# Five modulation chunks by VectorE: multiply and add on VectorE during the first feed-forward, TensorE only sums over partitions

## The chip, the cores and the metric

The kernel runs on one core of a Trainium2 chip. The metric is the device time of one execution in microseconds (us); smaller is better. Engines are named as the profile names them: PE is TensorE, PEld its weight loads, DVE is VectorE, ACT is ScalarE, POOL is GpSimd, SP is SyncE, whose queue issues nearly all DMAs here.

## The reference

Two transformer blocks on 256 latent tokens (the first block also carries 256 context tokens), width 1024, all in float32. What matters here is the head of the first block: a modulation vector of nine chunks of 1024 is made from two conditioning vectors, and scales, shifts and gates the layers. Chunk 2 gates the first feed-forward, chunks 3 to 5 belong to the attention layer, chunks 6 to 8 to the second feed-forward.

```python
mod_lat = (jax.nn.silu(c) @ w_mod[layer] + b_mod[layer])[:, None, :]
mod_ctx = (jax.nn.silu(c_ctx) @ w_mod[layer] + b_mod[layer])[None, None, :]
ml = jnp.split(mod_lat, N_MOD, axis=-1)
mc = jnp.split(mod_ctx, N_MOD, axis=-1)
x = x + 0.5 * ml[2] * swiglu(modulate(rms_norm(x, norm1_g[layer]), ml[0], ml[1]),
                              ffn1_w_in[layer], ffn1_w_out[layer])
```

`w_mod` is 1024 x 9216, 37.7 MB, and it is used for two rows only. `swiglu` is 1024 to 2 x 2816 and back to 1024, on 512 tokens.

## The kernel before

Activations lie feature-major: 128 features of a chunk on the partitions, tokens in the free dimension. All large weights come as a stream of **units** of 1 MB (128 x 2048 floats) into the two buffers of `raw`. To keep float32 precision, each unit is split: ACT copies it to `w_hi` in a rounded format (L477), DVE subtracts to `w_lo` (L829), each in two halves of 1024 columns, and PE makes three matmuls for each product (L1455 hi by hi, L1456 hi by the activations' lo, L1457 lo by hi). In the first feed-forward (ffn1) a unit is 48 matmuls of 512 columns. It has 34 units in three slabs: 8 units of input weights and 4 of output weights, the same again, then 6 and 4. After an input unit k, ACT makes the silu (L563), DVE the product (L967), ACT its rounded part `h_hi` (L565), DVE `h_lo` (L970, which counts the unit as drained). After an output unit DVE adds to `x` (L929). DVE and ACT work on the halves of unit k + 2 around that: the first half before unit k's results, the second half behind them.

The modulation is computed in **mod units**: a quarter of a chunk, 256 rows of `w_mod`, 1 MB, laid out as 2 x 4 pieces of 256 columns. For each piece PE multiplies a 128 x 32 block of `sc_pad` (two columns are the silus of `c` and `c_ctx`, the others zero) with the piece, into 32 partitions of a bank of `ps_a`; four pieces fill four groups of 32 partitions (function `mod`, L1430). After the four quarters of a chunk DVE transposes the bank in 32 x 32 blocks and adds the bias (`modulation`, L850 and L853). There are 36 mod units. The first 8 (chunks 1 and 0) stand ahead of ffn1. Of the other 28, numbered n = 0 to 27, one each **rides** behind the units 0 to 20 of ffn1 on PE (`riding`), and the last 7 stand between ffn1 and the next projection. Mod units land in four slots (`wide_scr` and `scr`); SP issues the load of mod unit n right behind the load of stream unit n + 2 and waits there until PE has finished mod unit n - 4 (`mod_done`).

The order on each engine is the order of the code; nothing reorders it. DVE and SP run ffn1 in hardware loops over two units, PE has it written out. Semaphores that matter: `w_lo_ready` (a half of `w_lo` is there), `unit_drained`, `halves_done` (PE has finished a half), `mod_unit_done`, `mod_turned` (the bank is transposed and free).

## Time and profile before

| | |
|---|---|
| time, median of 3 runs | 1341.02 us (1337.63 to 1341.87) |
| profiled execution: span from first to last instruction | 1338.6 us |
| profiled execution: own time beside its span | not listed apart; the span is 2.4 us under the median and inside the range of the runs |
| PE busy | 1290.6 us, 96% of the span |
| DVE busy | 724.0 us, 54% |
| ACT busy | 588.0 us, 44% |
| mean granted PE clock | 0.977 of full speed |
| DMA | 214.17 MB, 160 GB/s in the mean |

Busy times are of one execution. A busy engine matters only where others wait for it, so the chain of waits and the time line of the stretch in question say more than these shares. ffn1 lies between about 40 and 428 us of the span.

### The profile page before, as it was taken

The numbers are of one execution on the slowest core, as the hardware profiler recorded it, in microseconds if no ns is written. First come the engines' busy times: TensorE is split into PE (matmuls) and PEld (weight loads), VectorE is DVE, ScalarE is ACT, GpSimd is POOL, SyncE is SP. The second block draws the span as 40 slices with busy tenths as digits, with TensorE's granted clock in tenths as the row PEclk, the third lists the DMA queues.
The fourth block names the chain that finished last, engine by engine and source line by source line (L and its number), as shares of the span: only waits on it lengthen the run. The fifth ranks groups of instructions, "written<-read, shape, count | busy, mean of one in ns | idle before, by whom it ended". The sixth has DMA issues, their size and how long they took to land.

```text
span 1338.6 us, 23359 instructions
## 1 busy us (share of the span) xinstructions
PE 1290.6 (96%) x8912; PEld 1147.0 (86%) x8912; DVE 724.0 (54%) x1210; ACT 588.0 (44%) x884; POOL 62.4 (5%) x72
## 2 busy tenths in 40 slices
PE   5899999999999999999998999998999999999997
PEld 3677777778887699888998999997888889999997
DVE  2533333333334765776665555655657767666664
ACT  2443223421233436554434656545434565544542
POOL 1000000000001000000001000002011201000001
PEclk7899999999999999999998999998999999999998
DMA  9544444344223344432453555544432325455542
GB/s 388 222 182 151 175 185 185 150 173 186 92 75 136 137 158 141 143 122 99 157 180 134 219 189 188 188 170 144 158 127 95 98 92 185 162 189 189 188 163 88
DMA packets 30958, 214.17 MB, mean 160 GB/s; under 512 B 3376, under 2 KB 4656, under 8 KB 5936
## 3 DMA queue, kind: packets, MB, share of 16 engines
q1 hardware_dynamic: 30032, 209.73, 43.3%
q10 hardware_dynamic: 864, 3.56, 0.7%
q8 instruction: 45, 0.74, 0.2%
q14 instruction: 17, 0.14, 0.0%
HBM read 212.23 MB, written 1.05 MB: 159 GB/s over the span
## 4 chain that ended last, share of the span: by engine, by line
PE 87%; DVE 5%; ACT 4%; DMA 2%; issue 2%; DVEq 0%; ACTq 0%; SPq 0%
PE ps_u L1455 26%; PE ps_u L1456 25%; PE ps_u L1457 25%; PE ps_a L1430 2%; PE ps_a L1413 1%; PE ps_a L1402 1%; DMA scr<-in_mods 1%; ACT w_hi L477 1%; DMA raw<-in_stream 1%; DVE w_lo L829 1%; PE ps_a L1668 1%; DVE sq L885 1%; PE ps_a L1605 1%; PE ps_a L1590 1%; PE ps_a L1764 1%
## 5 line engine op out<-in xcount | busy, mean ns | idle before, releaser
L1455 PE MATMUL ps_u<-x_hi,w_hi 128*128 128x256 f32 (+1 forms) x1744 | 545.5, 313 | 14.4 <-DVE x_lo L896 10.7
L829 DVE TENSOR_TENSOR w_lo<-raw,w_hi 128x1024 fp32r<-128x1024 f32 x322 | 394.4, 1229 | 289.7 <-ACT w_hi L477 285.3
L1456 PE MATMUL ps_u<-x_lo,w_hi 128*128 128x256 f32 (+1 forms) x1744 | 537.5, 308 | 0.0
L1457 PE MATMUL ps_u<-x_hi,w_lo 128*128 128x256 f32 (+1 forms) x1744 | 536.9, 308 | 0.0
L477 ACT ACTIVATE w_hi<-raw 128x1024 fp32r<-128x1024 f32 x322 | 336.9, 1054 | 301.4 <-PE ps_u L1457 253.7
L1455 PEld LDWEIGHTS ps_u<-x_hi,w_hi 128*128 128x128 f32 x1744 | 335.6, 192 | 44.2 <-issue 24.6
L1457 PEld LDWEIGHTS ps_u<-x_hi,w_lo 128*128 128x128 f32 x1744 | 335.5, 192 | 15.6
L1456 PEld LDWEIGHTS ps_u<-x_lo,w_hi 128*128 128x128 f32 x1744 | 335.8, 193 | 15.1 <-issue 0.5
L1455 PE MATMUL ps_u<-h_hi,w_hi 128*128 128x256 f32 (+1 forms) x800 | 246.4, 308 | 0.9 <-DVE h_lo L970 0.5
L1456 PE MATMUL ps_u<-h_lo,w_hi 128*128 128x256 f32 (+1 forms) x800 | 245.2, 307 | 0.0
L1457 PE MATMUL ps_u<-h_hi,w_lo 128*128 128x256 f32 (+1 forms) x800 | 245.0, 306 | 0.0
L1455 PEld LDWEIGHTS ps_u<-h_hi,w_hi 128*128 128x128 f32 x800 | 152.8, 191 | 11.0 <-issue 2.9
L1457 PEld LDWEIGHTS ps_u<-h_hi,w_lo 128*128 128x128 f32 x800 | 152.8, 191 | 7.0
L1456 PEld LDWEIGHTS ps_u<-h_lo,w_hi 128*128 128x128 f32 x800 | 152.8, 191 | 6.7
L408 POOL TENSOR_TENSOR sq<-sq 128x512 f32<-128x512 f32 (+1 forms) x30 | 36.7, 1222 | 974.2 <-ACT sq L529 886.9
L967 DVE TENSOR_TENSOR t<-s,ps_u 128x512 f32<-128x512 f32 (+1 forms) x44 | 24.4, 554 | 92.7 <-ACT s L563 92.7
L563 ACT ACTIVATE s<-ps_u 128x512 f32<-128x512 f32 (+1 forms) x44 | 21.5, 488 | 99.6 <-PE ps_u L1457 99.4
L929 DVE SCALAR_TENSOR_TENSOR x<-ps_u,gate_half,x 128x256 f32<-128x256 f32 x72 | 30.4, 477 | 32.6 <-PE ps_u L1457 32.5
L970 DVE TENSOR_TENSOR h_lo<-t,h_hi 128x512 f32 (+1 forms) x44 | 24.6, 559 | 36.1 <-ACT h_hi L565 36.1
L565 ACT ACTIVATE h_hi<-t 128x512 f32 (+1 forms) x44 | 23.1, 525 | 37.7 <-DVE t L967 37.7
L477 ACT ACT_TABLE_LOAD x19 | 24.4, 1283 | 17.9 <-DMA raw<-in_stream 17.7
L1430 PE MATMUL ps_a<-wide_scr,sc_pad 128*32 128x256 f32 x288 | 23.7, 463 | 7.1 <-ACT sc_pad L493 6.9
(228 smaller groups left out, 803.0 us busy)
## 6 DMA issues: line engine op xcount, KB each, us to landing
raw<-in_stream SPq DMA_DIRECT2D x153, 1024.0 KB, 4.8
wide_scr<-in_mods SPq DMA_DIRECT2D x18, 1024.0 KB, 6.7
scr<-in_mods SPq DMA_DIRECT2D x18, 1024.0 KB, 6.8
raw<-in_stream SPq DMA_DIRECT2D x8, 768.0 KB, 4.1
x<-in_tokens ACTq DMA_DIRECT2D x2, 1024.0 KB, 14.8
wide_scr<-in_cmp_w SPq DMA_DIRECT2D x2, 1024.0 KB, 7.8
sq<-in_cmp_w SPq DMA_DIRECT2D x2, 1024.0 KB, 7.5
out<-x SPq DMA_DIRECT2D x4, 256.0 KB, 2.2
```

What stands on the lines that cost most here:

```text
L408: pool.tensor_tensor(sq[:, 0, 0:width], sq[:, 0, 0:width], sq[:, kc, 0:width], ALU.add).then_inc(sq_sums, 1)
L477: act.activation(w_hi[:, k % 2, cols], raw[:, k % 2, cols], ACT.Copy).then_inc(h_ready, 1)
L563: act.activation(s1[:, j, 0:n], bank(k + j, 0, n), ACT.Silu).then_inc(silu_done, 1)
L565: act.activation(h_hi[:, 2 * p + j, 0:n], t1[:, j, 0:n], ACT.Copy).then_inc(hh_done, 1)
L829: dve.tensor_tensor(w_lo[:, k % 2, cols], raw[:, k % 2, cols], w_hi[:, k % 2, cols].bitcast(F32), ALU.subtract).then_inc(l_ready, 1)
L929: ins = dve.scalar_tensor_tensor(x[:, m + t, cols], bank(b, t, n)[:, cols], gate(m + t, s), x[:, m + t, cols], ALU.mult, ALU.add)
L967: dve.tensor_tensor(t1[:, j, 0:n], s1[:, j, 0:n], bank(k + j, 1, n), ALU.mult)\
L970: dve.tensor_tensor(h_lo[:, 2 * p + (first + j), 0:n], t1[:, j, 0:n], h_hi[:, 2 * p + (first + j), 0:n].bitcast(F32), ALU.subtract).then_i ...
L1430: ins = pe.matmul(ps_a[rows, b, 0:MOD_COLS], sc_pad[:, 2 * quarter + kc, :], mod_slots[slot][:, lo:lo + MOD_COLS], start=(quarter == 0 and ...
L1455: pe.matmul(dst, wh, xh, start=(kc == 0), stop=False)
L1456: pe.matmul(dst, wh, xl, start=False, stop=False)
L1457: ins = pe.matmul(dst, wl, xh, start=False, stop=(kc == span - 1))
```

## The change

Of the 28 mod units after the front, the first 20 (chunks 2 to 6, n = 0 to 19) are no longer multiplied by PE. Behind its work on unit n of ffn1, DVE multiplies each of the mod unit's two tiles of 128 x 1024 by the silu value of its partition, once for each of the two conditioning vectors, and adds to a running sum in `sq`, which is idle then (`mod_products`, four instructions of 1024 columns for a mod unit, eight tiles for a chunk). When a chunk's four quarters are in, PE sums over the partitions with 8 matmuls whose weights are a column of ones (`mod_sum`, `one_col`), one unit later than the last products. DVE reads the bank another unit later. Mod unit 20 rides on PE behind unit 22, the last seven stand where they stood. DVE and SP have ffn1 written out now, and `modulation` of chunks 2 to 6 moves from behind the loops into the sequence, at units 5, 9, 13, 17 and 21.

```diff
@@ -37,8 +37,9 @@
 MOD_QUARTERS = 4
 MOD_FRONT = 2 * MOD_QUARTERS
 MOD_RIDE = N_MOD * MOD_QUARTERS - MOD_FRONT
-MOD_LATE = 7
+MOD_SUMMED = 5 * MOD_QUARTERS
 MOD_ROWS = 32
+MOD_BANKS = (0, 1, 2, 0, 1)
 MOD_COLS = KD * MOD_ROWS
...
@@ -125,6 +126,7 @@
+        one_col = sb("one_col", [P, 2, MOD_ROWS])
...
@@ -166,6 +168,7 @@
+        mod_sums = sq[:].rearrange("p (b v k) n -> p b v (k n)", b=2, v=2)
...
@@ -356,22 +361,23 @@
                 sp.wait_ge(mod_done, u - 3)
                 mod_load(u, u - 4)
             load(0, 1, KD)
-            def riding_load(p, n):
-                sp.wait_ge(mod_done, 4 * p + (MOD_FRONT + n - 3))
-                mod_load(4 * p + (MOD_FRONT + n), n % 4)
-
-            with sp.Fori(0, MOD_RIDE // 4 - 1) as p:
-                for j in range(4):
-                    load(2 * p, 2 + j, KD)
-                    riding_load(p, j)
-            for n in range(MOD_RIDE - 4, MOD_RIDE):
+            def riding_load(n):
+                if n < 4:
+                    sp.wait_ge(mod_done, MOD_FRONT + n - 3)
+                elif n < MOD_SUMMED + 4:
+                    sp.wait_ge(mod_added, 4 * (n - 3))
+                else:
+                    sp.wait_ge(mod_done, MOD_FRONT + n - MOD_SUMMED - 3)
+                mod_load(MOD_FRONT + n, n % 4)
+
+            for n in range(MOD_RIDE):
                 load(0, 2 + n, KD)
-                if n == MOD_RIDE - 4:
-                    riding_load(0, n)
+                if n <= MOD_RIDE - 4:
+                    riding_load(n)
             units(2 + MOD_RIDE, 4, SLABS[2])
             units(FIRST["k"], 2)
             for n in range(MOD_RIDE - 3, MOD_RIDE):
-                riding_load(0, n)
+                riding_load(n)
             run(FIRST["k"] + 2, FIRST["ffn2"])
             def cmp_weights(i):
...
@@ -815,10 +821,13 @@
+            dve.memset(one_col[:], 0.0).then_inc(ones_ready, 1)
-            dve.wait_ge(ones_ready, 3)
+            dve.wait_ge(ones_ready, 4)
+            for v in range(2):
+                dve.memset(one_col[:, v, v:v + 1], 1.0).then_inc(ones_ready, 1)
...
@@ -844,9 +853,30 @@
             dve.tensor_tensor(gg[:], vec[:, V_F1:V_F1 + KD], vec[:, V_MIX:V_MIX + KD], ALU.mult).then_inc(vec_ready, 1)
             turned_cols = turned[:].rearrange("p (t c) -> p t c", c=MOD_ROWS)[:, :, 0:2]
+            def mod_products(n):
+
+                chunk, quarter = divmod(n, MOD_QUARTERS)
+                dve.wait_ge(mod_landed[n % 4], LANDED * (n // 4 + 3))
+                if quarter == 0 and chunk >= 2:
+                    dve.wait_ge(mod_summed, chunk - 1)
+                w = mod_slots[n % 4].rearrange("p (k c) -> p k c", k=2)
+                for kc in range(2):
+                    for v in range(2):
+                        total_v = mod_sums[:, chunk % 2, v, :]
+                        by = sc_pad[:, 2 * quarter + kc, v:v + 1]
+                        if quarter == 0 and kc == 0:
+                            ins = dve.tensor_scalar(total_v, w[:, kc, :], by, None, ALU.mult)
+                        else:
+                            dve.wait_ge(mod_added, 4 * n + 2 * kc + v - 1)
+                            ins = dve.scalar_tensor_tensor(total_v, w[:, kc, :], by, total_v, ALU.mult, ALU.add)
+                        ins.then_inc(mod_added, 1)
+
             def modulation(c, chunk, b):
-                dve.wait_ge(mod_done, MOD_QUARTERS * (c + 1))
+                if 2 <= c < 2 + MOD_SUMMED // MOD_QUARTERS:
+                    dve.wait_ge(mod_summed, c - 1)
+                else:
+                    dve.wait_ge(mod_done, MOD_QUARTERS * (c + 1) - (0 if c < 2 else MOD_SUMMED))
                 dve.transpose(turned[:], ps_a[:, b, 0:MOD_COLS]).then_inc(mod_turned, 1)
                 dve.wait_ge(mod_turned, c + 1)
                 cols = slice(chunk * KD, (chunk + 1) * KD)
...
@@ -959,39 +989,44 @@
                 def gate(m, s):
                     return gate_half[:, i, m, s:s + 1]
-                def pairs(pr, k, c, count, first=0):
+                def pair(pr, k, c, m, j):
+                    split(pr, k + 2, 0)
+                    dve.wait_ge(silu_done, c + 1)
+                    dve.tensor_tensor(t1[:, j, 0:n], s1[:, j, 0:n], bank(k, 1, n), ALU.mult).then_inc(prod_done, 1)
+                    dve.wait_ge(hh_done, c + 1)
+                    dve.tensor_tensor(h_lo[:, m, 0:n], t1[:, j, 0:n], h_hi[:, m, 0:n].bitcast(F32), ALU.subtract).then_inc(drained, 1)
+                    split(pr, k + 2, 1)
+
+                def pairs(pr, k, c, count):
                     with dve.Fori(0, count // 2) as p:
                         for j in range(2):
-                            split(pr + p, k + j + 2, 0)
-                            dve.wait_ge(silu_done, c + 2 * p + (j + 1))
-                            dve.tensor_tensor(t1[:, j, 0:n], s1[:, j, 0:n], bank(k + j, 1, n), ALU.mult)\
-                               .then_inc(prod_done, 1)
-                            dve.wait_ge(hh_done, c + 2 * p + (j + 1))
-                            dve.tensor_tensor(h_lo[:, 2 * p + (first + j), 0:n], t1[:, j, 0:n],
-                                              h_hi[:, 2 * p + (first + j), 0:n].bitcast(F32), ALU.subtract).then_inc(drained, 1)
-                            split(pr + p, k + j + 2, 1)
+                            pair(pr + p, k + j, c + 2 * p + j, 2 * p + j, j)
                 def outs(pr, k, last):
                     for o in range(4):
                         out_step(pr, k, o, n, gate, last)
                 if n == NB:
-                    pairs(0, base, count, 4)
-                    modulation(2, 2, 0)
-                    gates_of(0, 2)
-                    pairs(0, base + 4, count + 4, 4, 4)
-                    modulation(3, 3, 1)
-                    dve.wait_ge(gate_ready, 1)
-                    outs(0, base + 8, False)
-                    modulation(4, 4, 2)
-                    scale_of(1, 4, V_N2)
-                    pairs(0, base + 12, count + 8, 4)
-                    modulation(5, 5, 0)
-                    pairs(0, base + 16, count + 12, 4, 4)
-                    modulation(6, 6, 1)
-                    outs(0, base + 20, False)
-                    pairs(0, base + 24, count + 16, SLABS[2])
-                    outs(0, base + 30, True)
+                    at = 0
+                    for chunks in SLABS:
+                        for u in range(chunks + 4):
+                            if u < chunks:
+                                pair(0, base + at + u, count + u, u, u % 2)
+                            else:
+                                if u == chunks and at == 0:
+                                    dve.wait_ge(gate_ready, 1)
+                                out_step(0, base + at + chunks, u - chunks, n, gate, chunks == SLABS[2])
+                            if at + u < MOD_SUMMED:
+                                mod_products(at + u)
+                            c, late = divmod(at + u - 2, MOD_QUARTERS)
+                            if late == MOD_QUARTERS - 1 and 0 <= c < MOD_SUMMED // MOD_QUARTERS:
+                                modulation(2 + c, 2 + c, MOD_BANKS[c])
+                                if c == 0:
+                                    gates_of(0, 2)
+                                if c == 2:
+                                    scale_of(1, 4, V_N2)
+                        at += chunks + 4
+                        count += chunks
                 else:
                     with dve.Fori(0, 2) as s:
                         pairs(s * 6, base, s * 8 + count, SLABS[0])
...
@@ -1431,10 +1466,21 @@
                                         start=(quarter == 0 and kc == 0), stop=(quarter == MOD_QUARTERS - 1 and kc == 1))
                 ins.then_inc(mod_done, 1)
-            def riding(n):
+            def late(n):
                 u = MOD_FRONT + n
                 c = u // MOD_QUARTERS
-                mod(u, 1 if c == N_MOD - 1 else (c - 2) % 3 if c < N_MOD - 2 else 0, u % MOD_QUARTERS, n % 4, LANDED * (n // 4 + 3), c - 1)
+                mod(u, 1 if c == N_MOD - 1 else 0, u % MOD_QUARTERS, n % 4, LANDED * (n // 4 + 3), c - 1)
+
+            def mod_sum(c):
+
+                pe.wait_ge(mod_added, 4 * MOD_QUARTERS * (c + 1))
+                pe.wait_ge(mod_turned, c if c >= 3 else 2)
+                for v in range(2):
+                    for g in range(P // MOD_ROWS):
+                        rows = slice(g * MOD_ROWS, (g + 1) * MOD_ROWS)
+                        ins = pe.matmul(ps_a[rows, MOD_BANKS[c], 0:MOD_COLS], one_col[:, v, :],
+                                        mod_sums[:, c % 2, v, g * MOD_COLS:(g + 1) * MOD_COLS], start=(v == 0), stop=(v == 1))
+                ins.then_inc(mod_summed, 1)
             def unit(pr, k, operand, n=S, kcs=KD, ready=None, b=None, lag=2, parts=1):
...
@@ -1490,8 +1536,11 @@
                                 unit(0, base + k + o, from_x(n), n, ready=normed(i))
                             else:
                                 unit(0, base + k + o, from_h(n), n, chunks, ready=drained_at(0, base + k) if o == chunks else None)
-                            if k + o < MOD_RIDE - MOD_LATE:
-                                riding(k + o)
+                            c, behind = divmod(k + o - 1, MOD_QUARTERS)
+                            if behind == MOD_QUARTERS - 1 and c < MOD_SUMMED // MOD_QUARTERS:
+                                mod_sum(c)
+                            if k + o == MOD_SUMMED + 2:
+                                late(MOD_SUMMED)
                 else:
                     with pe.Fori(0, 2) as s:
                         slab(s, s * 6, base, SLABS[0])
```

PE, between unit 3 and unit 4 of ffn1. Before, the eight matmuls of mod unit 3 stand there:

```order
L1455 MATMUL ps_u<-x_hi,w_hi 128x512
L1456 MATMUL ps_u<-x_lo,w_hi 128x512
L1457 MATMUL ps_u<-x_hi,w_lo 128x512
L1430 MATMUL ps_a<-scr,sc_pad 32x256 [waits mod_landed3]
L1430 MATMUL ps_a<-scr,sc_pad 32x256 x7
L1455 MATMUL ps_u<-x_hi,w_hi 128x512 [waits x_lo_ready,w_lo_ready,unit_drained]
```

The same place now (L1501 to L1503 are the three matmul lines):

```order
L1501 MATMUL ps_u<-x_hi,w_hi 128x512
L1502 MATMUL ps_u<-x_lo,w_hi 128x512
L1503 MATMUL ps_u<-x_hi,w_lo 128x512
L1501 MATMUL ps_u<-x_hi,w_hi 128x512 [waits x_lo_ready,w_lo_ready,unit_drained]
L1502 MATMUL ps_u<-x_lo,w_hi 128x512
```

PE now, between unit 4 and unit 5, the first of the five places with a `mod_sum`:

```order
L1502 MATMUL ps_u<-x_lo,w_hi 128x512
L1503 MATMUL ps_u<-x_hi,w_lo 128x512
L1481 MATMUL ps_a<-sq,one_col 32x256 [waits mod_turned,mod_products_added]
L1481 MATMUL ps_a<-sq,one_col 32x256 x7
L1501 MATMUL ps_u<-x_hi,w_hi 128x512 [waits x_lo_ready,w_lo_ready,unit_drained]
L1502 MATMUL ps_u<-x_lo,w_hi 128x512
```

So eight short matmuls stand behind every fourth unit instead of behind each, and they wait for DVE's products where the old ones waited for a DMA.

DVE, one unit of ffn1 before (the body of its loop; `t` and `s` are the product and the silu, REGISTER_ALU and ISA rows compute the loop's semaphore values):

```order
L829 TENSOR_TENSOR w_lo<-raw,w_hi 128x1024 [waits w_hi_ready]
L967 TENSOR_TENSOR t<-s,ps_u 128x512 [waits silu_done]
L970 ISA [waits h_hi_done]
L970 TENSOR_TENSOR h_lo<-t,h_hi 128x512
L828 REGISTER_ALU
L829 TENSOR_TENSOR w_lo<-raw,w_hi 128x1024 [waits w_hi_ready]
```

DVE now, unit 5, where a transposition follows too (L838 is `w_lo`, L995 and L997 are `t` and `h_lo`):

```order
L838 TENSOR_TENSOR w_lo<-raw,w_hi 128x1024 [waits w_hi_ready,unit_drained]
L995 TENSOR_TENSOR t<-s,ps_u 128x512 [waits silu_done]
L997 TENSOR_TENSOR h_lo<-t,h_hi 128x512 [waits h_hi_done]
L838 TENSOR_TENSOR w_lo<-raw,w_hi 128x1024 [waits w_hi_ready]
L871 SCALAR_TENSOR_TENSOR sq<-wide_scr,sc_pad,sq 128x1024 [waits mod_products_added,mod_landed1]
L871 SCALAR_TENSOR_TENSOR sq<-wide_scr,sc_pad,sq 128x1024 [waits mod_products_added] x3
L880 STREAM_TRANSPOSE turned<-ps_a 128x256 [waits mod_chunk_summed]
L883 TENSOR_TENSOR mods<-turned,vec 128x16 [waits mod_turned]
L895 TENSOR_SCALAR gate_half<-mods 128x16 [waits mods_ready]
```

The four new instructions stand behind the second half of `w_lo` and ahead of the first half for the next unit but one. In a chunk's first quarter two of the four are TENSOR_SCALAR, without a sum to add to.

## Rows read from the trace of the kernel before

**Rows 1.** The page: span, PE busy, and the chain of waits by engine

```profile
span 1338.6 us, 23359 instructions
PE 1290.6 (96%) x8912; PEld 1147.0 (86%) x8912; DVE 724.0 (54%) x1210; ACT 588.0 (44%) x884; POOL 62.4 (5%) x72
...
PE 87%; DVE 5%; ACT 4%; DMA 2%; issue 2%; DVEq 0%; ACTq 0%; SPq 0%
```

**Rows 2.** Busy by stretch: from:to, length, PE, PEld, DVE, ACT, POOL, clock, DMA share, GB/s

```profile
60.00:150.00 90.00, 90.00 (x471) 69.56 (x470) 29.30 (x34) 31.45 (x35) 0.00 (x0) 1.00 0.48 185
```

**Rows 3.** Time line of PE at mod unit 0: start, duration, instruction

```profile
53.42 1.07 PE L1430 MATMUL ps_a<-wide_scr,sc_pad 128*32 128x256 f32 x16
54.42 0.50 PE L1455 MATMUL ps_u<-x_hi,w_hi 128*128 128x512 f32 x1
```

**Rows 4.** Time line of ACT: the silus behind units 0, 7, 24 and 29

```profile
53.53 0.60 ACT L563 ACTIVATE s<-ps_u 128x512 f32<-128x512 f32 x1 [3.08 <-PE ps_u L1457]
...
138.55 0.60 ACT L563 ACTIVATE s<-ps_u 128x512 f32<-128x512 f32 x1 [4.38 <-PE ps_u L1457]
...
341.25 0.60 ACT L563 ACTIVATE s<-ps_u 128x512 f32<-128x512 f32 x1 [4.38 <-PE ps_u L1457]
...
395.65 0.60 ACT L563 ACTIVATE s<-ps_u 128x512 f32<-128x512 f32 x1 [4.38 <-PE ps_u L1457]
```

**Rows 5.** Time line of PE: mod unit 21 and, back to back, 22 and 23

```profile
428.18 1.07 PE L1430 MATMUL ps_a<-wide_scr,sc_pad 128*32 128x256 f32 x16
...
429.07 1.91 PE L1430 MATMUL ps_a<-scr,sc_pad 128*32 128x256 f32 x32
```

**Rows 6.** Time line of DVE: behind unit 0, and the end of chunk 2's transposition

```profile
54.16 0.69 DVE L967 TENSOR_TENSOR t<-s,ps_u 128x512 f32<-128x512 f32 x1 [3.75 <-ACT s L563]
55.78 0.69 DVE L970 TENSOR_TENSOR h_lo<-t,h_hi 128x512 f32 x1 [0.93 <-ACT h_hi L565]
56.59 1.23 DVE L829 TENSOR_TENSOR w_lo<-raw,w_hi 128x1024 fp32r<-128x1024 f32 x1
61.33 1.23 DVE L829 TENSOR_TENSOR w_lo<-raw,w_hi 128x1024 fp32r<-128x1024 f32 x1 [3.51 <-ACT w_hi L477]
...
94.18 0.44 DVE L850 STREAM_TRANSPOSE turned<-ps_a 128x256 f32<-128x256 f32 x1
...
94.86 0.17 DVE L865 TENSOR_SCALAR gate_half<-mods 128x16 f32<-128x16 f32 x1
```

**Rows 7.** Groups of DVE by form, whole span: busy, mean ns of one, idle before

```profile
L829 DVE TENSOR_TENSOR w_lo<-raw,w_hi 128x1024 fp32r<-128x1024 f32 x322 | 394.4, 1229 | 289.7 <-ACT w_hi L477 285.3 <-DVE q_cur L1369 0.6
...
L970 DVE TENSOR_TENSOR h_lo<-t,h_hi 128x256 f32 x22 | 9.4, 426 | 15.7 <-ACT h_hi L565 15.7
...
L1114 DVE TENSOR_SCALAR scr<-scr,inv 128x512 f32<-128x512 f32 x16 | 7.1, 484 | 0.3
...
L1121 DVE SCALAR_TENSOR_TENSOR t<-u_pad,vec,t 128x256 f32<-128x256 f32 x8 | 3.9, 484 | 0.7 <-DVE t L1119 0.5
```

**Rows 8.** Time line of DVE: two halves of `w_lo` with no wait between

```profile
28.49 2.36 DVE L829 TENSOR_TENSOR w_lo<-raw,w_hi 128x1024 fp32r<-128x1024 f32 x2
```

**Rows 9.** Time line of PE around the `w_lo` at 61.33

```profile
60.26 0.39 PE L1456 MATMUL ps_u<-x_lo,w_hi 128*128 128x512 f32 x1
...
61.40 0.39 PE L1455 MATMUL ps_u<-x_hi,w_hi 128*128 128x512 f32 x1
...
62.53 0.39 PE L1457 MATMUL ps_u<-x_hi,w_lo 128*128 128x512 f32 x1
```

**Rows 10.** SP's issues behind unit 0, and DMA issues by line with KB and us to landing

```profile
57.99 0.33 SPq L336 DMA_DIRECT2D raw<-in_stream  x1
58.58 0.33 SPq L350 DMA_DIRECT2D scr<-in_mods  x1
...
raw<-in_stream SPq DMA_DIRECT2D x153, 1024.0 KB, 4.8
```

**Rows 11.** Time line at the start: PE's first mod matmuls

```profile
6.95 1.93 PE L1430 MATMUL ps_a<-wide_scr,sc_pad 128*32 128x256 f32 x16 [6.95 <-ACT sc_pad L493]
```

12 lines of the change are left out of this document (7 added, 5 removed).

## The prediction

> **What bounds the kernel now.** I read the page first: PE is busy for 1290.6 of 1338.6 us, and the chain that ended last runs over PE for 87% of the span [rows 1]. A busy PE alone would prove little, so I read the stretch that the change touches. From 60 to 150 us PE is busy for 90.00 of 90.00 us at a granted clock of 1.00, which is the 2.4 GHz level, while DVE is busy for 29.30 and ACT for 31.45 [rows 2]. The reader is to see one engine without a gap and two others with two thirds of their time free. In this stretch a microsecond taken from PE is a microsecond of the kernel, as long as nobody else becomes late.
>
> How PE's time divides shows in the silus of ACT, which follow the end of each input unit at once. From unit 0 to unit 7, each with a mod unit riding, seven periods take 138.55 - 53.53 = 85.02 us, 12.146 each. From unit 24 to unit 29, with no mod unit, five periods take 395.65 - 341.25 = 54.40, 10.88 each [rows 4]. The units are the same 48 matmuls, so a riding mod unit costs PE 12.146 - 10.88 = **1.266 us**. That is more than the 1.00 us from its first matmul to the next unit's first [rows 3], since the stream of large matmuls also stops and restarts; the difference of periods holds all of it.
>
> **What is removed and added on PE.** Before, 21 mod units ride in the first feed-forward; 20 of them go (n = 0 to 19), and the 21st stays, behind unit 22 instead of unit 20: moved, at the same price. Removed: 20 x 1.266 = 25.3 us. Added: five sums. Each has 8 matmuls of the same form, 32 output rows by 256 columns in four groups of partitions, and stands alone between two units like a mod unit. I take the same 1.266 us: 6.3 us. From below the bound is the cost where such blocks follow each other: 429.07 - 428.18 = 0.89 us [rows 5], in all 4.5 us. From above I add 1 us of waiting for each, in all 11.3 us. I take the price of the ride, because a sum interrupts the stream in just the way a ride does. Net: 25.3 - 6.3 = **19.0 us**, between 14.0 and 20.9.
>
> **What is added on DVE, and what hides it.** Let T be the end of a unit on PE, 53.42 for unit 0 [rows 3]. DVE then makes the product at T + 0.74, `h_lo` until T + 3.05 and the second half of `w_lo` until T + 4.40; after that it is idle until ACT's next `w_hi`, which lets it go on at T + 7.91 [rows 6]. The four new instructions go into that hole. There is no such row of 1024 columns. The nearest is `w_lo`, two inputs and 1024 columns: 1229 ns. A SCALAR_TENSOR_TENSOR with the scalar read from SBUF takes 484 ns for 256 columns where a TENSOR_TENSOR takes 426, so 58 ns more [rows 7]: 1.29 us for one. Two `w_lo` with no wait between take 2.36 us, so the second adds 1.13, 0.1 less than its duration [rows 8]; the pitch of the new ones is then 1.19 and the block of four 3 x 1.19 + 1.29 = 4.86 us. The bound from above is that the whole price goes with the width, 4 x 484 = 1.94 us each; the bound from below is 484 ns for a TENSOR_SCALAR of 512 columns, 0.97 us for twice that [rows 7], which 10 of the 80 instructions may well come near. I take 1.19, by the row of the same width.
>
> The block ends at T + 4.3 + 4.86 = T + 9.2. The transposition that follows at five places takes 95.03 - 94.18 = 0.85 us with its two small companions [rows 6]: T + 10.0. Then comes the first half of the next `w_lo`, 1.13 us: T + 10.3, or T + 11.2 at the five places. DVE's next product is due at 10.88 + 0.74 = T + 11.62. So DVE is on time in each unit, by 1.3 us, at the worst by 0.4. Even late it would not stop PE at once. PE's unit k + 2 needs `h_lo` of unit k, which is done at T + 3.05 and due at T + 10.88, so PE forgives about 7.8 us of lag.
>
> Three queues are touched by moved waits. **PE:** the sum of a chunk waits for the products of the unit before the last. They end at T + 9.2, and PE arrives at T + 10.88, so the wait is met 1.7 us early; behind it on PE stands the whole next unit, and everybody waits for that. **SP:** the load of mod unit n waits for the products of n - 4 instead of PE's mod unit n - 4, and the next stream load is queued behind it. SP comes to it at 58.58, right after the stream load at 57.99 [rows 10], T + 5.2 of unit n - 2, and the products of n - 4 were done over 17 us before. No change, also for the DMAs' times. The stream load at T + 4.6 lands after 4.8 us [rows 10] and ACT needs it in the middle of the unit after next, about T + 17.7, so the shorter period leaves 8 us. **DVE:** the transposition waits for a sum that PE made at least the length of a unit earlier.
>
> At nothing I cost the three more small memsets at the start (PE's first mod matmul comes at 6.95 us and waited for ACT [rows 11], far behind DVE's memsets), and the code written out where there were loops on DVE and SP; both have idle time ahead of their next wait. If that cover were gone, a few tenths of a microsecond would be at stake.
>
> Will a busier DVE slow PE's reads? Five matmuls from 60.26 to 61.40 take 1.14 us before the `w_lo` at 61.33, five from 61.40 to 62.53 take 1.13 under it [rows 9]. No.
>
> **The sum.** The profiled execution has a span of 1338.6 us, 2.4 under the median of the runs shown. 1338.6 - 19.0 = 1319.6 us of span; with the same 2.4 around it **1322.0 us**, which is 1341.02 - 19.0, 1.4% faster.
>
> **Rivals.**
> *TensorE waits for VectorE at the sums.* The 1.7 us of reserve vanish if the pitch passes (10.88 - 4.3) / 4 = 1.65 us, or if a block begins 1.7 us late. Against it: the idle time of DVE in [rows 6]. For it: the price of the new instruction is inferred from other widths. With 1 us for each of the five places the gain is 14.0 us: 1327 us.
>
> *VectorE becomes the bound, and the kernel slower.* A unit with no idle time costs DVE 1.13 + (56.59 + 1.23 - 54.16) = 4.79 us [rows 6, 8] and four pitches p. Twenty units and five transpositions: 20 x 4.79 + 5 x 0.85 + 80 p = 100 + 80 p. Less the 7.8 us of lag it must stay under PE's 20 x 10.88 + 6.3 = 223.9 us, so PE loses from p = 1.65, and the gain is used up at p = 1.88, where it reaches the 242.9 us of before. At the upper bound of 1.94 it is 247.4: 4.5 us slower, 1345.5 us. Against it stands the 1229 ns row, for it only that no wide SCALAR_TENSOR_TENSOR is in the trace.
>
> *Each VectorE instruction holds the next one for its own length again.* Then p = 2 x 1.29 = 2.58, DVE needs 100 + 206 - 7.8 = 298.6 us, and the kernel takes 1341 + 56 = 1397 us. The pair of `w_lo` in 2.36 us [rows 8] speaks against it: held like that it would take 3.7 or more. The Trainium skill, VectorE: DVE Perf Modes, section The DRAIN you can't avoid, says that a flush of roughly the duration less 266 ns follows every op and that the next op starts only then. By that rule, an estimate: p = 1.29 + 1.02 = 2.31, and the kernel would come out near 1375 us. The trace disagrees for two `w_lo` in a row.
>
> *The matmuls go, the time does not.* If something else paced the units, the weights for example, PE would wait where it now multiplies, and the time would stay at 1341. Against it: units 24 to 29 already run at 10.88 us with the same stream loads [rows 4], though with less DMA beside them.
>
> **How the numbers follow.** The forecast has 85 in 100. PE waiting at the sums has 6, DVE as the bound at its upper price 4, the doubled hold 2, no effect 3. The likeliest case alone runs from 1320 (sums at 0.89 us) to 1323; the runs of before lie up to 3.4 us under their median, so its low end is 1318. To the first rival the range reaches 1327. That leaves out 9 in 100 and what I have not thought of. About 0.3%, 4 us, is what a measurement of this kernel can tell from no change. Faster: 85 + 6 = 91; same: 3; slower: 4 + 2 = 6.
>
> **What the profile after would show.** Periods of 10.88 us between silus, and 12.15 where a sum stands; L1465 in 16 mod units (8 in front, 8 late) and L1481 in five blocks; L871 at about 1.29 us; DVE about 80% busy in the stretch and still with a short idle time ahead of each product; no wait of PE for DVE at L1481; the rest of the span 19 us earlier and otherwise the same. The prediction fails if L871 takes over 1.65 us, if L1481 shows a wait, or if the large matmuls are further apart than 0.227 us while DVE multiplies.

## The result, and the profile after

The changed kernel takes **1323.94 us** (median of 4 runs, 1322.94 to 1324.6), the kernel before 1340.9 on the same chip: a ratio of 0.9876, 95% interval 0.9863 to 0.9889. The forecast was 1322.0 in a range of 1318 to 1327. The profiled execution took 1324.6 us; its span is 15.8 us shorter than the one before [rows 1].

The page of the changed kernel: span, busy times, the chain by engine.

```profile
span 1322.8 us, 22749 instructions
...
PE 1273.7 (96%) x8688; PEld 1143.5 (86%) x8688; DVE 813.5 (61%) x1293; ACT 588.4 (44%) x884; POOL 62.6 (5%) x72
...
PE 88%; DVE 5%; ACT 3%; DMA 2%; issue 1%; DVEq 0%; SPq 0%; ACTq 0%
```

PE is busy for 16.9 us less, DVE for 89.5 us more, and DVE's share of the chain is what it was: the new work is paid out of idle time. Busy times by stretch, in the columns of [rows 2]:

```profile
60.00:150.00 90.00, 90.00 (x419) 73.12 (x418) 67.77 (x70) 32.97 (x37) 0.00 (x0) 1.00 0.51 196
415.00:419.00 4.00, 4.00 (x36) 2.05 (x36) 1.05 (x5) 0.26 (x1) 0.00 (x0) 0.57 1.01 426
739.00:744.00 5.00, 4.74 (x27) 4.77 (x28) 3.49 (x6) 2.97 (x5) 0.00 (x0) 0.66 0.43 139
910.00:928.00 18.00, 12.99 (x54) 11.36 (x55) 8.60 (x23) 6.85 (x16) 3.38 (x2) 0.53 0.18 60
```

In the first of them PE still has no gap, with DVE at 75%. The other three come back below. The time line of DVE behind unit 1 shows the block of new instructions and what stands around it (line 838 was 829, 995 was 967, 997 was 970):

```profile
65.58 0.69 DVE L995 TENSOR_TENSOR t<-s,ps_u 128x512 f32<-128x512 f32 x1 [3.63 <-ACT s L569]
67.07 0.69 DVE L997 TENSOR_TENSOR h_lo<-t,h_hi 128x512 fp32r<-128x512 f32 x1 [0.81 <-ACT h_hi L571]
68.02 1.23 DVE L838 TENSOR_TENSOR w_lo<-raw,w_hi 128x1024 fp32r<-128x1024 f32 x1 [0.26 <-ACT w_hi L483]
69.17 4.86 DVE L871 SCALAR_TENSOR_TENSOR sq<-wide_scr,sc_pad,sq 128x1024 f32<-128x1024 f32 x4
73.95 1.22 DVE L838 TENSOR_TENSOR w_lo<-raw,w_hi 128x1024 fp32r<-128x1024 f32 x1
76.46 0.69 DVE L995 TENSOR_TENSOR t<-s,ps_u 128x512 f32<-128x512 f32 x1 [1.29 <-ACT s L569]
```

The four take 4.86 us and begin without a wait; DVE then waits 1.29 us for the next silu. The instructions of lines 868, 871 and 1481 (min/median/max ns, first and last start us), and what PE waited for at 1481 (us, times):

```profile
L868 DVE TENSOR_SCALAR sq<-wide_scr,sc_pad x10: 746/747/748, 57.0 to 236.8; 128x1024 f32<-128x1024 f32 x10
L871 DVE SCALAR_TENSOR_TENSOR sq<-scr,sc_pad,sq x40: 1274/1278/1282, 80.0 to 273.7; 128x1024 f32<-128x1024 f32 x40
L1481 PE MATMUL ps_a<-sq,one_col x96: 379/379/404, 52.7 to 277.3; 128*32 128x256 f32 x96
  issue: 2.1, 6
```

The sums are not five but **six**: 96 records in blocks of 16, and the first stands at 52.70, ahead of every product; the one between units 4 and 5 is the second. The time line of PE shows it behind unit 0, and that of ACT gives the periods:

```profile
52.70 1.07 PE L1481 MATMUL ps_a<-sq,one_col 128*32 128x256 f32 x16
...
52.80 0.60 ACT L569 ACTIVATE s<-ps_u 128x512 f32<-128x512 f32 x1 [2.89 <-PE ps_u L1503]
64.95 0.60 ACT L569 ACTIVATE s<-ps_u 128x512 f32<-128x512 f32 x1 [4.38 <-PE ps_u L1503]
75.83 0.60 ACT L569 ACTIVATE s<-ps_u 128x512 f32<-128x512 f32 x1 [3.08 <-PE ps_u L1503]
...
377.19 0.60 ACT L569 ACTIVATE s<-ps_u 128x512 f32<-128x512 f32 x1 [4.38 <-PE ps_u L1503]
```

The period behind unit 0 is 12.15 us, the next 10.88. From the first to the last silu the feed-forward took 342.12 us [rows 4] and takes 324.39: 17.73 less, which is 14 x 1.266, for 20 rides removed and six sums added. The code says why. In `mod_sum`'s place PE asks, with `MOD_QUARTERS` = 4:

```python
c, behind = divmod(k + o - 1, MOD_QUARTERS)
if behind == MOD_QUARTERS - 1 and c < MOD_SUMMED // MOD_QUARTERS:
    mod_sum(c)
```

At k + o = 0 that is divmod(-1, 4) = (-1, 3), and the condition holds with c = -1. Eight matmuls sum a chunk that does not exist. I had read "one unit later than the last products" and counted chunks, not the cases in which the condition holds. The stray sum also advances `mod_summed` by one, so each of DVE's waits for a sum is already met by the sum before it. The data stay in order only because DVE's work on unit 4c + 5 waits for PE's results of that unit, which stand behind the sum of chunk c.

That leaves a second question. The feed-forward gave 17.73 us and the start 0.73 (this part is chance: the first silu starts between 52.16 and 53.96 us in the traces of this case, 53.50 and 52.75 in two of one and the same kernel), but the span fell by only 15.8. ACT has the same number of instructions in both kernels, so the start of one instruction in both, late in the program, gives what has been gained up to there. Time lines of ACT in the changed kernel, where the kernel before has the first of them at 439.31, the second at 757.60 and the third at 946.01:

```profile
420.86 1.31 ACT L525 ACTIVATE x_hi<-sq,mods 128x256 fp32r<-128x256 f32 x3 [5.27 <-DVE sq L915]
...
740.24 0.36 ACT L569 ACTIVATE s<-ps_u 128x256 f32<-128x256 f32 x1
...
930.69 1.06 ACT L483 ACTIVATE w_hi<-raw 128x1024 fp32r<-128x1024 f32 x1 [0.76 <-PE ps_u L1503]
```

Gained: 18.45 us, then 17.36, then 15.32. The gain gets lost in code that was not changed, and at places where the granted clock stands at its lower level (0.5, 1.2 GHz): the window from 739 to 744 shows 0.66, while before the window from 750 to 760, which holds the second instruction, had 1.00; and the low stretch from 910 to 928 is longer than its counterpart before (0.68 in the mean from 905 to 932, against 0.75 from 918 to 945). The low stretch at 415 loses nothing against the kernel before, which has the same one behind its own feed-forward:

```profile
433.00:437.00 4.00, 4.00 (x39) 2.04 (x38) 1.05 (x5) 0.26 (x1) 0.00 (x0) 0.58 1.01 426
```

### The profile page after: what moved, and what is told of

Its sections match the earlier page's. It is cut to its first block, busy times and chain, and to the rows that moved or that the text cites. A ratio compares the mean times of both kernels' runs of the same rounds, so it can differ in the third digit from the quotient of the medians.

```text
span 1322.8 us, 22749 instructions
## 1 busy us (share of the span) xinstructions
PE 1273.7 (96%) x8688; PEld 1143.5 (86%) x8688; DVE 813.5 (61%) x1293; ACT 588.4 (44%) x884; POOL 62.6 (5%) x72
## 3 DMA queue, kind: packets, MB, share of 16 engines
q10 hardware_dynamic: 864, 3.56, 0.7%
## 4 chain that ended last, share of the span: by engine, by line
PE 88%; DVE 5%; ACT 3%; DMA 2%; issue 1%; DVEq 0%; SPq 0%; ACTq 0%
PE ps_u L1501 26%; PE ps_u L1502 26%; PE ps_u L1503 26%; PE ps_a L1448 1%; PE ps_a L1437 1%; DMA scr<-in_mods 1%; PE ps_a L1717 1%; DMA raw<-in_stream 1%; DVE w_lo L838 1%; PE ps_a L1465 1%; ACT w_hi L483 1%; DVE sq L915 1%; PE ps_a L1654 1%; PE ps_a L1639 1%; PE ps_a L1813 1%
## 5 line engine op out<-in xcount | busy, mean ns | idle before, releaser
L1501 PE MATMUL ps_u<-x_hi,w_hi 128*128 128x256 f32 (+1 forms) x1744 | 544.2, 312 | 15.0 <-DVE x_lo L926 10.4
L1503 PE MATMUL ps_u<-x_hi,w_lo 128*128 128x256 f32 (+1 forms) x1744 | 537.4, 308 | 0.0
L838 DVE TENSOR_TENSOR w_lo<-raw,w_hi 128x1024 fp32r<-128x1024 f32 x322 | 393.8, 1227 | 220.1 <-ACT w_hi L483 218.4
L1501 PEld LDWEIGHTS ps_u<-x_hi,w_hi 128*128 128x128 f32 x1744 | 336.2, 193 | 39.7 <-issue 20.8
L1503 PEld LDWEIGHTS ps_u<-x_hi,w_lo 128*128 128x128 f32 x1744 | 336.3, 193 | 15.4
L1501 PE MATMUL ps_u<-h_hi,w_hi 128*128 128x256 f32 (+1 forms) x800 | 246.0, 308 | 0.7 <-DVE h_lo L1417 0.7
L1503 PE MATMUL ps_u<-h_hi,w_lo 128*128 128x256 f32 (+1 forms) x800 | 245.1, 306 | 0.0
L1501 PEld LDWEIGHTS ps_u<-h_hi,w_hi 128*128 128x128 f32 x800 | 152.8, 191 | 9.7 <-issue 2.2
L1503 PEld LDWEIGHTS ps_u<-h_hi,w_lo 128*128 128x128 f32 x800 | 152.8, 191 | 6.9
L995 DVE TENSOR_TENSOR t<-s,ps_u 128x512 f32<-128x512 f32 (+1 forms) x44 | 24.4, 554 | 65.3 <-ACT s L569 65.3
L871 DVE SCALAR_TENSOR_TENSOR sq<-scr,sc_pad,sq 128x1024 f32<-128x1024 f32 x40 | 48.7, 1278 | 0.0
L997 DVE TENSOR_TENSOR h_lo<-t,h_hi 128x512 fp32r<-128x512 f32 (+1 forms) x44 | 24.6, 559 | 33.3 <-ACT h_hi L571 33.3
L871 DVE SCALAR_TENSOR_TENSOR sq<-wide_scr,sc_pad,sq 128x1024 f32<-128x1024 f32 x30 | 36.7, 1278 | 0.0
```

Source lines behind the costliest of these rows:

```text
L838: dve.tensor_tensor(w_lo[:, k % 2, cols], raw[:, k % 2, cols], w_hi[:, k % 2, cols].bitcast(F32), ALU.subtract).then_inc(l_ready, 1)
L871: ins = dve.scalar_tensor_tensor(total_v, w[:, kc, :], by, total_v, ALU.mult, ALU.add)
L995: dve.tensor_tensor(t1[:, j, 0:n], s1[:, j, 0:n], bank(k, 1, n), ALU.mult).then_inc(prod_done, 1)
L997: dve.tensor_tensor(h_lo[:, m, 0:n], t1[:, j, 0:n], h_hi[:, m, 0:n].bitcast(F32), ALU.subtract).then_inc(drained, 1)
L1501: pe.matmul(dst, wh, xh, start=(kc == 0), stop=False)
L1503: ins = pe.matmul(dst, wl, xh, start=False, stop=(kc == span - 1))
```

## The experiments

Each was timed beside the kernel before, whose median then lay between 1337.7 and 1340.1; ratios are to that. Line numbers of an edited kernel can differ by a few.

**Five sums.** The condition becomes what the text of the change says.

```diff
-                            if behind == MOD_QUARTERS - 1 and c < MOD_SUMMED // MOD_QUARTERS:
+                            if behind == MOD_QUARTERS - 1 and 0 <= c < MOD_SUMMED // MOD_QUARTERS:
```

> The changed kernel makes six sums, not five: the condition for a sum also holds behind unit 0, for a chunk number of -1. Here it asks for a chunk number of at least 0, nothing else differs. Theory (a sum costs a ride's 1.27 us wherever it stands, even when it sums nothing useful): the period between the silus behind units 0 and 1 falls from 12.15 to 10.88 us, all the others stay, and the time falls by 1.3 us, to about 1322.7. Rival (the long first period is the start of the first feed-forward, not the sum): the period stays at 12.15 and so does the time.

Measured: 1318.26 us (1317.96 to 1319.31), ratio 0.9844 (0.9831 to 0.9858), span 1317.5. Its windows at the places above, its ACT instructions (those of the three rows above), and its first periods:

```profile
415.00:419.00 4.00, 2.89 (x34) 0.97 (x26) 2.20 (x7) 1.10 (x3) 0.00 (x0) 1.00 1.00 422
739.00:744.00 5.00, 5.00 (x44) 5.00 (x43) 1.60 (x2) 2.91 (x3) 0.00 (x0) 1.00 0.69 259
907.00:921.00 14.00, 10.42 (x43) 8.79 (x43) 6.13 (x20) 4.48 (x10) 1.69 (x2) 0.51 0.22 75
992.00:996.00 4.00, 3.38 (x17) 3.29 (x17) 3.97 (x10) 1.01 (x2) 3.61 (x4) 0.57 0.01 4
```

```profile
52.75 0.60 ACT L569 ACTIVATE s<-ps_u 128x512 f32<-128x512 f32 x1 [2.95 <-PE ps_u L1503]
63.63 0.60 ACT L569 ACTIVATE s<-ps_u 128x512 f32<-128x512 f32 x1 [4.37 <-PE ps_u L1503]
...
417.90 1.31 ACT L525 ACTIVATE x_hi<-sq,mods 128x256 fp32r<-128x256 f32 x3 [3.63 <-DVE sq L915]
...
736.36 0.36 ACT L569 ACTIVATE s<-ps_u 128x256 f32<-128x256 f32 x1
...
925.07 1.06 ACT L483 ACTIVATE w_hi<-raw 128x1024 fp32r<-128x1024 f32 x1 [0.71 <-PE ps_u L1503]
```

Behind unit 0 the period is 10.88 now: the sixth sum cost 1.27 us there. The whole is 5.7 us faster by the medians (4.3 by the ratios, since the kernel before also came out 1 us lower beside it), not 1.3. The changed kernel is behind it by 2.96 us at the first instruction, 3.88 at the second, 5.62 at the third. Beyond the 1.27 us, each step lies at a stretch where the changed kernel's clock was at 1.2 GHz and this one's was not, or not as long: the mod units and the statistics at 415 (0.57 against 1.00; DVE's `sq` there comes 1.64 us sooner for ACT), 739 to 744 (0.66 against 1.00), 18 us against 14 at 910. It has a low stretch at 992 that the changed kernel has not, and the spans at the end differ by 5.3 us. So 1.3 us of the 5.7 are work, and most of the rest goes with the clock. What the clock costs can be read from the same two mod units on PE, first in the kernel before, then in five sums:

```profile
433.68 3.56 PE L1430 MATMUL ps_a<-wide_scr,sc_pad 128*32 128x256 f32 x32
...
413.89 1.93 PE L1465 MATMUL ps_a<-wide_scr,sc_pad 128*32 128x256 f32 x32
```

That is 1.63 us. Five sums save it against the kernel before too, which makes their gain larger than the work taken away.

**The changed kernel and five sums, again.** Both as they were, timed side by side.

> The changed kernel unchanged, beside the other kernels of this call on one chip, since e1 came out 5.7 us faster than it and not 1.3, on another day's rows. Theory (beyond the 1.27 us of the sixth sum, the difference is TensorE's granted clock, which in the profile of the changed kernel was at 1.2 GHz for 3.4 us around 416 us and not in e1's, and longer around 910): 1322 to 1325 again, 4 to 6 us over five sums. Rival (a difference of chips): it comes within 2 us of the repeated e1.

> Five sums once more, beside the changed kernel. Theory: 1317 to 1320. Rival (chance): over 1321.

Measured: 1324.94 us (1321.67 to 1325.32), 0.9887 (0.9872 to 0.9902), and 1318.48 us (1317.83 to 1321.61), 0.9844 (0.983 to 0.9859). At two places the clock repeats with the kernel: from 415 to 419 it is 0.57 and 1.00, from 735 to 745 it is 0.83 and 1.00, as in the first executions. There it belongs to the kernel, not to one execution. It is not so further on: from 905 to 932 the changed kernel shows 0.68 in its first trace and 0.81 in this one, and five sums have no low stretch at 992 this time. Of the third step, and of the order in which single spans come out, a part is therefore chance of the execution. The difference itself is not: 6.5 us by the medians, 5.8 by the ratios.

**The sixth block elsewhere.** Five sums, and eight matmuls of the same form behind unit 21, for which nobody waits; their result is used by nobody.

```diff
+                            if k + o == MOD_SUMMED + 1:
+                                pe.wait_ge(mod_turned, 5)
+                                for v in range(2):
+                                    for g in range(P // MOD_ROWS):
+                                        rows = slice(g * MOD_ROWS, (g + 1) * MOD_ROWS)
+                                        pe.matmul(ps_a[rows, 2, 0:MOD_COLS], one_col[:, v, :],
+                                                  mod_sums[:, 0, v, g * MOD_COLS:(g + 1) * MOD_COLS], start=(v == 0), stop=(v == 1))
```

> Five sums' kernel with one block of the same eight matmuls more, but behind unit 21 instead of behind unit 0; its result is used nowhere. All that follows the first feed-forward is then shifted by 1.27 us, as in the changed kernel. Theory (the 1.27 us shift decides where TensorE's clock falls later, so the sixth sum costs 1.27 us directly and some 4 more through the clock): about 1324, with the clock at 1.2 GHz around 416 us and between 735 and 745 us. Rival (what costs the rest is the block's place behind unit 0): about 1319.7, with the clock at 2.4 GHz in both stretches.

Measured: 1325.23 us (1322.72 to 1325.92), 0.9899 (0.9879 to 0.9919). The time does not hang on the block's place behind unit 0: one such block costs 6.8 us against five sums again by the medians, 7.4 by the ratios. My theory was half right about the clock: from 415 to 419 it is 1.00 and not low, from 735 to 745 it is 0.83. In its profile, which is of its fastest execution, ACT also waits 2.7 us for a stream load, until 1142.7 us. So "the clock falls at 415" is not the whole of it; that the time ends up where the changed kernel's is, is shown, and by which stretches, differs.

**Each sum made twice.** The same eight matmuls again, into the same bank: the second time starts the bank anew (`start` for v = 0) and replaces the first, so the result is the same.

```diff
-                for v in range(2):
+                for v in (0, 1, 0, 1):
```

> Five sums' kernel with the eight matmuls of each sum made twice, back to back, into the same bank; the second time replaces the first. Theory (1.27 us is mostly the price of eight matmuls at 0.89 us, the rest that of the interruption, which is paid once): the five long periods grow by 0.89 us, from 12.15 to 13.04, and the time by 4.5 us, more or less what the clock does. Rival (the interruption is the price and matmuls pile up for little): they grow by less than 0.5 us.

Measured: 1322.52 us (1321.77 to 1326.76), 0.989 (0.9868 to 0.9912). The period with a sum goes from 12.15 to 12.96 us (silus at 96.05 and 109.01): another block of eight, right behind the first, costs 0.81, in all 4.1 us. The time is 4.0 us above five sums again, which was timed apart from it; by the ratios to the kernel before (0.989 against 0.9844) it is 6.2. Both are inside the intervals, so this run doesn't tell whether a shift of 4.1 us costs only what it adds. In its trace the clock is low around 420 us (0.83 from 415 to 425) and 1.00 from 735 to 745. The sixth block elsewhere was timed beside it, and there the kernel with 2.8 us less work on PE came out 2.7 us slower by the medians: work on PE alone does not order these kernels.

**All seven chunks.** `MOD_SUMMED = 7 * MOD_QUARTERS`, two banks more in the list, no late mod unit on PE, the loads of the last three in the loop with the others.

```diff
-MOD_SUMMED = 5 * MOD_QUARTERS
+MOD_SUMMED = 7 * MOD_QUARTERS
...
-MOD_BANKS = (0, 1, 2, 0, 1)
+MOD_BANKS = (0, 1, 2, 0, 1, 2, 0)
...
-            for n in itertools.islice(late_units, 3):
-                late(n)
             stat(1, 4)
-            for n in itertools.islice(late_units, 2):
-                late(n)
             spread(1, 4)
-            for n in late_units:
-                late(n)
```

> On top of five sums: all seven chunks behind the front go over VectorE, products behind units 0 to 27, sums behind every fourth unit up to 28, so TensorE has no mod unit between the first feed-forward and the next projection. In the feed-forward there are 7 sums at 1.27 us, one interruption more than with five sums and a ride. Theory (the late mod units lie on the path where the spread of the norm's roots stands behind two of them in TensorE's queue): the stretch from the last output unit to the first matmul of the projection, 13.1 us before, gets about 2 us shorter, and the time falls by 2 less 1.3, plus nothing else, to about 1321 to 1322. First rival (the late mod units only fill waits): the time goes up by one interruption, about 1323. Second rival (without them TensorE idles long enough for its clock to fall to 1.2 GHz there): a stretch at the low clock of some us more, time 1324 or more.

Measured: 1323.99 us (1322.61 to 1325.97), 0.989 (0.9874 to 0.9906), 5.7 slower than five sums, beside which it was timed, with less work on PE. Windows behind the feed-forward, and PE's time line there:

```profile
410.00:413.00 3.00, 0.67 (x3) 0.21 (x2) 2.29 (x5) 0.59 (x2) 0.00 (x0) 1.00 0.00 0
413.00:430.00 17.00, 12.45 (x39) 9.67 (x40) 9.77 (x27) 7.18 (x16) 0.00 (x0) 0.51 0.17 62
```

```profile
413.09 4.96 PE L1445 MATMUL ps_a<-ones,sq 128*128 128x1 f32 x24 [2.41 <-ACT sq L532]
```

The late mod units had filled the time in which PE waits for the statistics of the next norm. Without them PE idles 2.41 us, and what it does next runs at 1.2 GHz for 17 us.

**Six chunks.** The same edit with 6; of the last four mod units, three stand ahead of the statistics and one between them and their spreading.

```diff
-MOD_SUMMED = 5 * MOD_QUARTERS
+MOD_SUMMED = 6 * MOD_QUARTERS
...
-            late_units = iter(range(MOD_SUMMED + 1, MOD_RIDE))
+            late_units = iter(range(MOD_SUMMED, MOD_RIDE))
```

> Five sums' kernel, with chunk 7 over VectorE too: six sums, no ride, and of the seven late mod units on TensorE the four of chunk 8 stay. Three of them stand ahead of the statistics, where TensorE waits for the squares, and one, instead of two, ahead of the spread. In the feed-forward TensorE does the same as with five sums and one ride. Theory (seven chunks were slow because TensorE had nothing to do while it waited for the squares and its clock fell for 17 us): with the three units back the clock stays at 2.4 GHz there, and the time is that of five sums or 0.4 us less, since the spread no longer stands behind two units. Rival (VectorE's work in the last slab is what made seven chunks slow): two thirds of the loss stay, about 1322.

Measured: 1318.4 us (1317.66 to 1320.05), 0.9839 (0.9825 to 0.9852): the same as five sums. The clock fell here too, against the hope that one chunk's mod units would be cover enough:

```profile
412.00:415.00 3.00, 3.00 (x35) 2.40 (x34) 0.66 (x4) 0.26 (x1) 0.00 (x0) 1.00 0.76 248
415.00:426.00 11.00, 7.54 (x19) 4.77 (x16) 8.42 (x23) 6.11 (x12) 0.00 (x0) 0.53 0.07 28
```

**Half as much again on VectorE.** With five sums, behind each of the 80 new instructions one more of 512 columns, into a buffer that nobody reads then.

```diff
                         ins.then_inc(mod_added, 1)
+                        for e in range(1):
+                            at = (4 * n + 2 * kc + v) * 1 + e
+                            if at:
+                                dve.wait_ge(more_done, at)
+                            dve.scalar_tensor_tensor(q_cur[:].rearrange('p a n -> p (a n)'), w[:, kc, 0:NB], by, w[:, kc, NB:2 * NB], ALU.mult, ALU.add).then_inc(more_done, 1)
```

> Five sums, and behind each of the 80 products one more VectorE instruction of 512 columns whose result nobody uses: about 0.65 us of pitch each, 2.6 us a unit. VectorE then needs 100 + 80 x 1.19 - 5 (the 10 products without a sum are cheaper) + 52 = 242 us for the 20 units, more than TensorE's 224. Theory A, the prediction's (TensorE forgives 7.8 us of lag): TensorE loses 242 - 8 - 224 = 10 us in the feed-forward. Theory B (the sum forgives only the 1.7 us between the end of the products and the end of the next unit, and gives the lag back to TensorE at each of its places): TensorE loses about 16 us, and it waits at the sums, not at the units.

Measured once: 1348.63 us. From the first to the last silu 348.08 us instead of 323.12: 24.96 more, while the expectations had 10 and 16. The waits from 50 to 400 us (us in total, times, longest), and DVE's products at units 2 to 5:

```profile
PEld ps_a L1487 <- DVE sq L872: 16.0, 5, 4.0
PE ps_a L1487 <- DVE sq L872: 13.9, 5, 3.6
```

```profile
77.66 0.68 DVE L1001 TENSOR_TENSOR t<-s,ps_u 128x512 f32<-128x512 f32 x1
89.80 0.68 DVE L1001 TENSOR_TENSOR t<-s,ps_u 128x512 f32<-128x512 f32 x1
101.94 0.68 DVE L1001 TENSOR_TENSOR t<-s,ps_u 128x512 f32<-128x512 f32 x1
115.98 0.69 DVE L1001 TENSOR_TENSOR t<-s,ps_u 128x512 f32<-128x512 f32 x1 [2.90 <-ACT s L570]
```

DVE's period is 12.14 us, 1.3 longer than PE's. PE never waits for `h_lo` in this stretch; it waits at all five sums. At the first of them DVE's product, at 101.94, is 4 us late (the silu starts at 97.32, and the product follows a silu by 0.63 us when DVE is free), well under 7.8. And the wait has a second price, in the windows around the first of them:

```profile
98.00:100.00 2.00, 0.00 (x0) 0.00 (x0) 2.00 (x3) 0.00 (x0) 0.00 (x0) 0.91 0.99 418
100.00:106.00 6.00, 5.73 (x25) 3.69 (x26) 4.95 (x7) 1.58 (x2) 0.00 (x0) 0.50 0.00 1
```

After a wait of 3 us PE multiplies for 6 us at 1.2 GHz. That DVE itself waits 2.90 us for a silu behind the sum shows that it is PE that is slow by then. Four of the five waits last 3.0 to 3.6 us, and each has such a stretch behind it; the one before the sum at 199.44 us lasts 0.3, and the clock stays at 1.00. 13.9 us are the waits; I put the remaining 11 down to the four stretches at half the clock, 6 us or so each, and to the restarts.

**Twice as much on VectorE.** The same with two such instructions.

> Two more instructions behind each product: 5.2 us a unit more than with five sums alone. VectorE needs 100 + 95 - 5 + 104 = 294 us for the 20 units. Theory A: TensorE loses 294 - 8 - 224 = 62 us. Theory B: 68 us, with waits at the sums. Rival (the period of a unit is not set by VectorE's sum of work but by a chain through ScalarE, which waits for VectorE too): clearly more than 70 us.

Measured once: 1398.6 us, 77.2 more between the first and the last silu; expected were 62, 68 and over 70. Waits from 50 to 460 us, and two instructions of DVE at the ends of a block:

```profile
PE ps_a L1487 <- DVE sq L872: 53.5, 5, 14.7
PE ps_u L1507 <- DVE h_lo L1003: 10.0, 2, 5.3
...
72.40 1.28 DVE L872 SCALAR_TENSOR_TENSOR sq<-wide_scr,sc_pad,sq 128x1024 f32<-128x1024 f32 x1
...
82.98 1.22 DVE L839 TENSOR_TENSOR w_lo<-raw,w_hi 128x1024 fp32r<-128x1024 f32 x1
```

DVE is the bound for most of the stretch (busy for 82.80 of the 90 us from 60 to 150, PE for 75.26). A block of four products and eight extra instructions takes 82.98 - 72.40 = 10.58 us, so p is 2.65, and my formula 100 + 80p gives 312 us, 306 with the ten cheaper products counted as such. Against PE's 223.9 that is 82 us more, or 75 with 7.8 us forgiven; 77.2 lies between, so the total doesn't tell the two theories apart. The waits do: 53.5 us of them stand at the five sums and 10.0 at `h_lo`.

**The code written out, alone.** The kernel before with DVE's loops over pairs of units, in both feed-forwards, as loops of the generating program.

```diff
-                    with dve.Fori(0, count // 2) as p:
+                    for p in range(count // 2):
```

> The kernel before, only with VectorE's loops over the units of both feed-forwards written out. Theory (VectorE has idle time ahead of each wait, so loop arithmetic costs nothing): 1338 to 1341, ratio 1.000 with an interval around it. Rival (part of the change's gain comes from the written-out code): faster by 1 us or more, and shorter periods between silus than 12.146 us.

Measured: 1339.81 us (1336.72 to 1341.05, 11 runs), ratio 1.0001 (0.9991 to 1.001). It neither costs nor gives anything that could be measured.

**Rides and products.** VectorE makes all 80 products, PE rides all 20 mod units as before, and there is no sum; the products are used by nobody. The waits of SP and DVE are adapted; of the edit only PE's part is shown.

```diff
-                            c, behind = divmod(k + o - 1, MOD_QUARTERS)
-                            if behind == MOD_QUARTERS - 1 and c < MOD_SUMMED // MOD_QUARTERS:
-                                mod_sum(c)
+                            n_ride = k + o
+                            if n_ride < MOD_SUMMED:
+                                c = (MOD_FRONT + n_ride) // MOD_QUARTERS
+                                mod(MOD_FRONT + n_ride, (c - 2) % 3, n_ride % MOD_QUARTERS, n_ride % 4, LANDED * (n_ride // 4 + 3), c - 1)
```

> VectorE makes all 80 products as in the changed kernel, but TensorE still rides all 20 mod units and no sum is made; the products are used by nobody. Theory A (VectorE's 80 instructions of 1.28 us cost TensorE nothing, neither by waits nor by slower matmuls or copies): periods between silus 12.15 us as in the kernel before, the kernel as before, 1338 to 1342 us. Rival B (they cost something that the removal of the rides has hidden, through SBUF or through VectorE's lag): periods over 12.25 us, the kernel 1344 us or more.

Measured: 1340.52 us (1337.63 to 1343.14, 10 runs), ratio 1.0002 (0.9991 to 1.0012). The window shows PE without a gap and DVE with twice its work of [rows 2]:

```profile
60.00:150.00 90.00, 90.00 (x483) 69.05 (x481) 61.31 (x63) 31.05 (x35) 0.00 (x0) 1.00 0.47 178
```

The first period is 12.15 us (silus at 52.16 and 64.31), as before. So the whole load on VectorE is free here, and the gain of the change is what leaves PE. That it is free at the shorter period too is shown by the changed kernel: its 10.88 us with products is that of the units without a mod unit before [rows 4].

## Why the prediction was right, and where it was not

**The mechanism was right, and so were the sizes.** PE had no gap in the stretch, work taken from it came back in full as shorter periods, and DVE's new work went into its idle time. A block on PE costs 1.27 us when it stands alone, a ride (the 17.73 us) as well as a sum (12.15 less 10.88). A wide product takes 1278 ns where I had 1290, four take 4.86 us as forecast, and the block ends at 69.17 + 4.86 = 74.03, 9.2 us after unit 1's end, which is 0.11 before the silu at 64.95, as in [rows 3, 4]. DVE's reserve of 1.3 us is there in the row at 76.46. The large matmuls stay 0.227 us apart while DVE multiplies (23 pitches from 68.83 to 74.04 us). DVE is busy for 75% of the stretch where I had about 80%: the two first products of each chunk, 747 ns, are cheaper.

**"Added: five sums" was mis-sized.** It was six: 7.6 us in place of 6.3, and 17.7 in place of 19.0. The row at 52.70 shows the sixth, and five sums show what it costs directly. The statement that there are five blocks at L1481 fell with it.

**"The rest of the span 19 us earlier and otherwise the same" failed.** Of 18.45 us gained, 3.1 were gone at 930 us. I had no term for the clock. The two spans differ by 15.8 us, the medians by 17.0; how much of the 3.1 us a typical execution loses, the single profiles don't tell. The loss at 740 is in both traces of the changed kernel, the longer stretch at 910 in one of them.

**That 1322.0 came within 2 us is partly luck.** The forecast was added up for five sums. The kernel with five sums takes 1318.3 us, at the very edge of the range; by the ratio (0.9844) it gains 20.9 us where I had 19.0, and 1.6 of that comes from the low stretch at 415, which the kernel before has and it has not. The sixth sum and the clock, neither of which I had thought of, brought the changed kernel back up to near the forecast, on its other side. The upper part of the range was meant for waits at the sums, and there were none.

**"PE forgives 7.8 us of lag" was wrong.** That holds for the wait on `h_lo` alone. The sum of a chunk needs the products of the unit before, and there the reserve is 1.7 us (T + 10.88 less T + 9.2), as the same paragraph had it for the wait. The two extra-work kernels show the lag paid mostly at the sums (13.9 us of waits there and none at `h_lo`, then 53.5 and 10.0). For this change it made no difference, since DVE was never late; but the turning point of the second rival was off: without the 7.8 us it lies at p = (223.9 - 100) / 80 = 1.55, not 1.65.

**The rivals.** No wait of PE for DVE stands at L1481 in the changed kernel, so the first did not happen, and with p = 1.19 nor did the second. The third, the doubled hold, is out: with it four products would take 3 x 2.56 + 1.28 = 8.96 us, and 4.86 are measured. The Trainium skill, VectorE: DVE Perf Modes, section The DRAIN you can't avoid, would put the starts of two such products 2.3 us apart (an estimate from its "duration less 266 ns") if each were held until the flush is over. The same section also says that a next op which is not held starts earlier, which the prediction left out; the trace shows such an earlier start, with (4.86 - 1.28) / 3 = 1.19 us from start to start. The fourth, no effect, is contradicted by the silus at 10.88.

**What was costed at nothing was nothing.** DVE's written-out code (ratio 1.0001) is shown alone. VectorE's load beside the matmuls is shown with everything else of the change but the sums and the missing rides, SP's written-out code, its waits and the memsets included (1.0002), so none of these costs anything that could be measured, unless two of them cancel.

**The better version.** Five sums, 1318.3 and 1318.5 us, beats the kernel before by 1.6% and the changed one by 0.4 to 0.5%. Six chunks are as fast and no faster.

**What stays open.** Why a shift of 1.3 us in the feed-forward brings the lower clock at 415 or 740 (both in the changed kernel, 740 alone with the block behind unit 21), while one of 4.1 us has it around 420 and not at 740, and costs 4.0 to 6.2 in all. That the clock differs there is shown; what tips it is not, and no run set the clock by itself. For the sixth block elsewhere the profile has a low stretch at 740 and one late stream load, and I can't divide the 7 us between them.

## What to carry to other kernels

Count instructions added by a condition by running through its first and last cases, or count them in the build, not by the sentence that describes them; `divmod` of a negative number is one such case. A reserve is that of the nearest wait in time, so each new semaphore needs a reserve of its own, and the largest one found elsewhere on the engine says nothing. If idle time of another engine is the currency, first give it the work with nothing taken away, as in rides and products: a ratio of 1 says that the currency is real. And compare a kernel with a copy shifted by a microsecond before you trust a difference of 0.4%.
